# Two 128-token tiles taken one after the other through norms, turns and dense products

## The chip, the cores and the metric

The kernel runs on one NeuronCore of a Trainium2 chip. Its engines run in parallel, each through its own list of instructions in order: TensorE (PE in the rows, with PEld for its weight loads), VectorE (DVE), ScalarE (ACT), GpSimd (POOL), and SyncE (SP), whose list issues most of the DMA transfers. They wait for each other through semaphores. The metric is the time of one execution on the device, in microseconds (us); for one core that is the time of that core. All data is float32.

## The reference

256 tokens of width 1024 pass two blocks and then a third. Block 0 mixes by moving averages (pool), block 1 by a gated delta rule (GDN), both followed by a squared-ReLU MLP and a gated embedding; the third has attention of several kinds, a mixture of 32 experts and a last gated embedding.

```python
for i in range(2):
    mix = pool_mixer(x, ...) if i == 0 else gated_deltanet(x, ...)
    x = layer_norm(ALPHA * x + mix, ln_gain[i, 0], ln_bias[i, 0])
    ff = square(relu(x @ mlp_w1[i])) @ mlp_w2[i]            # 1024 -> 4096 -> 1024
    pe = sigmoid(x @ ple_gate_w[i] + ple_gate_b[i]) * (p[i] @ ple_proj[i])
    x = layer_norm(ALPHA * x + ff + pe, ln_gain[i, 1], ln_bias[i, 1])
x += attention(rmsnorm(x, ln1));  x += experts(rmsnorm(x, ln2))
x += sigmoid(rmsnorm(x, ln_ple) @ gate) * (p2 @ proj);  out = rmsnorm(x, ln_f)
```

A layer norm needs the mean and variance over the 1024 values of a token, an RMS norm the mean square. Both work on each token by itself, and so does every dense product.

## The kernel before

The 256 tokens are two tiles of 128, tile 0 and tile 1, one token to a partition. `x`, `pre` and `side` are (128, 2, 1024) arrays in SBUF: partition, tile, column. `ps` is all of PSUM, four pairs of banks of 1024 columns. `ring` has six slots for weights (2 MB each), filled by SyncE; `row_buf` has three slots for a broadcast row (a gain, a bias), filled in turn by GpSimd as `row_used` lets it go.

**A norm and a turn.** A dense product wants its input with the columns on the partitions, so after a norm TensorE transposes both tiles (`pe_transpose`, L477, 8 transposes a tile) into PSUM pairs 0 and 1. Pair 0 gets columns 0 to 511 of both tiles and pair 1 the rest, so both copies to `xT` wait for tile 1: VectorE copies pair 0 (L483), ScalarE pair 1 (L487). I call this a turn. There are eight: `ln00`, `ln01`, `gdny`, `ln10`, `rn1`, `att`, `rn2`, `rnp`. In `v_layer_norm` VectorE first takes the statistics of both tiles (L430 to L432), then for each tile subtracts the mean and multiplies by the gain (L437), takes the reciprocal of the standard deviation that ScalarE made (L440), and scales and adds the bias (L441). An RMS norm has its square and root on ScalarE (L468, L469) and two VectorE steps (L456, L457).

**Dense products.** `pe_dense` (L498) multiplies `xT` by two ring slots of weights, tile 0 and then tile 1. TensorE runs a float32 product as two passes, and the trace has a record for each: 32 records of 128x512 a tile. It serves the two embedding gates (`pe_ple`, followed by the embedding product L552, 8 records a tile), GDN's and attention's output products and the last gate.

**The MLP.** Eight steps of 512 hidden columns. A step is an up product (four chunks of weights), a turn of its 128x512 squares (L668), and a down product (four chunks). Each float32 product is split into three products of fp32r halves (L591 to L593). ScalarE makes the high half of each chunk of weights (L758) and VectorE the low half (L709), into four buffers. TensorE's order is up(s+1) chunk 0, turn(s), up(s+1) chunks 1 to 3, down(s). A step's turn and the making of its halves so lie beside the next step's up product. The first step and the last have no such neighbour. In every chunk both tiles are computed.

**Order of the stages** on TensorE: pool products (L511, L520); turn, gate and embedding products, MLP of block 0; turn `ln01`, the small products for GDN's gates (L847, 16 columns), six units of GDN input products (L866, 256 columns, both tiles at once); the delta rule; turn `gdny`, GDN output product, norm and turn `ln10`, gate and embedding products, MLP of block 1; norms `ln11` and `rn1`, attention input (L1274); attention; turn `att`, output product; norm and turn `rn2`, router (L1667); experts; the last embedding product (L1764), turn `rnp`, last gate, last norm, output. The order is written out by hand in one function for each engine.

## Time and profile before

| | us |
|---|---|
| median of 3 runs (2198.16 to 2199.28) | 2199.13 |
| the profiled execution, its own time | 2196.63 |
| its span, first to last instruction | 2194.8 |
| TensorE busy (92% of the span) | 2022.3 |
| VectorE busy (32%) | 702.3 |
| ScalarE busy (19%) | 425.7 |

The mean granted clock of TensorE is 0.941 of full speed. The profiled execution is 2.50 us under the median; 1.83 us of its time lie outside its span. In a row of a timeline the first number is the start in us from the span's start, the second the duration in us (of a merged group, from its first start to its last end), then engine, line, operation, output and inputs, form and count, and in brackets the idle time of that engine before it and what ended it.

### The profile page before, as it was taken

The numbers are of one execution on the slowest core, as the hardware profiler recorded it, in microseconds if no ns is written. First come the engines' busy times: TensorE is split into PE (matmuls) and PEld (weight loads), VectorE is DVE, ScalarE is ACT, GpSimd is POOL, SyncE is SP. The second block draws the span as 40 slices with busy tenths as digits, with TensorE's granted clock in tenths as the row PEclk, the third lists the DMA queues.
The fourth block names the chain that finished last, engine by engine and source line by source line (L and its number), as shares of the span: only waits on it lengthen the run. The fifth ranks groups of instructions, "written<-read, shape, count | busy, mean of one in ns | idle before, by whom it ended". The sixth has DMA issues, their size and how long they took to land.

```text
span 2194.8 us, 22402 instructions
## 1 busy us (share of the span) xinstructions
PE 2022.3 (92%) x8722; PEld 1219.0 (56%) x8722; DVE 702.3 (32%) x980; ACT 425.7 (19%) x648; POOL 12.8 (1%) x20
## 2 busy tenths in 40 slices
PE   5899989989799996977789999999999999999997
PEld 3588778579347885866454343444435344444433
DVE  4355433275335543035221312122221221222132
ACT  1244412112124442015210011011101010101002
POOL 0000000000000000000000000000000000000000
PEclk8999979989899998967889999999999999999998
DMA  9245421300433344110448999999899999989972
GB/s 367 115 176 208 176 112 39 115 1 0 172 144 153 153 190 183 66 50 1 175 182 353 422 408 382 409 378 422 363 423 408 378 409 376 422 365 422 384 305 96
DMA packets 67807, 543.32 MB, mean 248 GB/s; under 512 B 7552, under 2 KB 7552, under 8 KB 10528
## 3 DMA queue, kind: packets, MB, share of 16 engines
q1 hardware_dynamic: 65296, 533.53, 59.7%
q0 software_dynamic: 2160, 7.87, 1.1%
q8 instruction: 44, 0.72, 0.1%
q10 hardware_dynamic: 288, 1.05, 0.1%
q14 instruction: 19, 0.16, 0.0%
HBM read 541.37 MB, written 1.05 MB: 247 GB/s over the span
## 4 chain that ended last, share of the span: by engine, by line
PE 90%; DVE 6%; ACT 2%; issue 1%; DMA 0%; DVEq 0%; SPq 0%; ACTq 0%
PE ps L1889 15%; PE ps L1875 10%; PE ps L1904 8%; PE ps L498 7%; PE ps L591 6%; PE ps L592 6%; PE ps L593 6%; PE ps L1918 5%; PE ps L866 4%; PE ps L1072 3%; PE ps L1274 3%; PE ps L1980 2%; PE ps L1967 1%; PE ps L874 1%; PE ps L1949 1%; PE ps L1279 1%
## 5 line engine op out<-in xcount | busy, mean ns | idle before, releaser
L1889 PE MATMUL ps<-ring,arena 128*64 128x512 f32 x1536 | 334.9, 594 | 0.0
L1889 PEld LDWEIGHTS ps<-ring,arena 128*64 128x64 f32 x1536 | 108.2, 137 | 214.3 <-issue 214.3
L591 PE MATMUL ps<-ring_split,arena_split 128*128 128x512 f32 x512 | 208.5, 407 | 18.4 <-DVE ring_split L709 15.8
L1875 PE MATMUL ps<-ring,arena 128*128 128x512 f32 x512 | 224.0, 596 | 0.0
L2112 DVE TENSOR_SCALAR arena<-ps 128x512 f32<-128x512 f32 x40 | 27.7, 692 | 601.7 <-PE ps L1889 344.6
L592 PE MATMUL ps<-ring_split,arena_split 128*128 128x512 f32 x512 | 206.1, 403 | 0.0
L593 PE MATMUL ps<-ring_split,arena_split 128*128 128x512 f32 x512 | 205.9, 402 | 0.0
L709 DVE TENSOR_TENSOR ring_split<-ring,ring_split 128x1024 fp32r<-128x1024 f32 x128 | 155.3, 1223 | 115.0 <-ACT ring_split L758 114.9
L1904 PE MATMUL ps<-ring,arena 128*64 128x512 f32 x768 | 170.1, 595 | 0.0
L1875 PEld LDWEIGHTS ps<-ring,arena 128*128 128x128 f32 x512 | 97.8, 191 | 117.2 <-issue 115.9
L758 ACT CAST ring_split<-ring 128x1024 fp32r<-128x1024 f32 x128 | 132.7, 1049 | 118.5 <-PE ps L593 108.0
L498 PE MATMUL ps<-ring,xT 128*128 128x512 f32 x320 | 145.2, 616 | 5.7 <-ACT xT L487 5.7
L2243 ACT ACTIVATE arena<-arena 128x512 f32<-128x512 f32 x40 | 25.2, 631 | 593.2 <-DVE arena L2112 593.2
L591 PEld LDWEIGHTS ps<-ring_split,arena_split 128*128 128x128 f32 x512 | 98.6, 193 | 44.3 <-issue 17.1
L1918 PE MATMUL ps<-ring,arena 128*128 128x512 f32 x256 | 111.9, 595 | 2.5 <-DVE x L2133 2.5
L593 PEld LDWEIGHTS ps<-ring_split,arena_split 128*128 128x128 f32 x512 | 98.5, 192 | 24.1
L592 PEld LDWEIGHTS ps<-ring_split,arena_split 128*128 128x128 f32 x512 | 98.8, 193 | 23.2
L1904 PEld LDWEIGHTS ps<-ring,arena 128*64 128x64 f32 x768 | 53.0, 137 | 104.7 <-issue 104.7
L498 PEld LDWEIGHTS ps<-ring,xT 128*128 128x128 f32 x320 | 62.9, 198 | 85.8 <-issue 79.9
L2133 DVE SCALAR_TENSOR_TENSOR x<-ps,side,x 128x512 f32<-128x512 f32 x128 | 87.0, 742 | 1.9 <-PE ps L1949 1.9
L866 PE MATMUL ps<-xT,ring 128*128 128x256 f32 x384 | 85.9, 387 | 0.9 <-DVE arena L960 0.9
L2146 DVE TENSOR_TENSOR arena_split<-ps,arena_split 128x512 fp32r<-128x512 f32 x40 | 26.9, 690 | 186.1 <-ACT arena_split L2257 186.1
(360 smaller groups left out, 1982.6 us busy)
## 6 DMA issues: line engine op xcount, KB each, us to landing
ring<-experts_dram SPq DMA_DIRECT2D x384, 1024.0 KB, 10.7
ring<-weights_dram SPq DMA_DIRECT2D x57, 2048.0 KB, 9.0
row_buf<-rows_dram POOLq DMA_DIRECT2D x15, 512.0 KB, 5.8
ring<-weights_dram SPq DMA_DIRECT2D x3, 1024.0 KB, 11.6
tab<-tables_dram SPq DMA_DIRECT2D x1, 2285.0 KB, 17.9
x<-tokens_dram SPq DMA_DIRECT2D x1, 1024.0 KB, 5.0
arena<-rows_dram SPq DMA_DIRECT2D x2, 512.0 KB, 19.0
xT<-weights_dram SPq DMA_DIRECT2D x1, 1024.0 KB, 7.0
```

Source lines behind the costliest of these rows:

```text
L498: m = T.matmul(ps[:, pair_of[t], half * 512:half * 512 + 512], xT[:, k, t * P:(t + 1) * P], ring[:, slot, at:at + 512], start=(k == 0), st ...
L591: T.matmul(out_, high, w_high, start=start, stop=False, skip_group_check=True)
L592: T.matmul(out_, high, w_low, start=False, stop=False, skip_group_check=True)
L593: return T.matmul(out_, low, w_high, start=False, stop=stop, skip_group_check=True)
L709: V.tensor_tensor(low, raw, high, ALU.subtract).then_inc(sem("mlp_low"), 1)
L758: A.copy(split_buffer(MLP_SPLIT_SLOT, buffer)[0], raw).then_inc(sem("mlp_high"), 1)
L866: m = T.matmul(ps[:, n % 4, b * SEQ:(b + 1) * SEQ], w[:, k * STEP + b * P:k * STEP + (b + 1) * P], xT[:, k, :], start=(k == 0), stop=(k == ...
L1875: ins = T.matmul(bank(2 * half_ + m), xs_big[:, 2 * c + d, :], w[:, d, m * STEP:(m + 1) * STEP], start=False, stop=c == 3 and d == 1, skip ...
L1889: ins = T.matmul(bank(first_bank + m)[at:at + SMALL], xs_small[:, 2 * c + d, SMALL * (j - 1):SMALL * j], w[half_][:, d, m * STEP:(m + 1) * ...
L1904: ins = T.matmul(bank(to)[at:at + SMALL], actT[:, 0, f % 4, SMALL * (f // 4):SMALL * (f // 4 + 1)], w[:, d, half_ * STEP:(half_ + 1) * STE ...
L1918: ins = T.matmul(bank(4 + half_), actT[:, f // 4, f % 4, :], w[:, d, half_ * STEP:(half_ + 1) * STEP], start=f == 0, stop=f == 7, skip_gro ...
L2133: V.scalar_tensor_tensor(out=part, in0=bank(banks[i]), scalar=weight_s[:, t, bass.ds(k, 1)], in1=part, op0=ALU.mult, op1=ALU.add).then_inc ...
```

## The change

Everything that stood between two big products for both tiles now goes tile by tile, with semaphores of their own for each tile (`norm_x0`, `norm_x1` and so on).

- **Turns.** `pe_transpose` puts tile t into PSUM pair t. Tile 0 is copied by ScalarE alone, in two copies of 512 columns; tile 1 by VectorE (first half) and ScalarE (second half).
- **Norms.** `v_layer_norm` finishes tile 0 before it begins tile 1, the sum before the norm (`produce`) among it. For `ln11` the following RMS norm of tile 0 is put between.
- **Products.** Dense products of tile 0 start when tile 0 is turned. The first unit of GDN's and of attention's input product is done as 128 + 128 columns instead of 256; GDN's small products come after its first unit.
- **Embedding product.** In block 0 it comes before the gate products, right behind the pool products, and its weights are loaded ahead of the gate's; in block 1 between tile 0's and tile 1's gate products.
- **MLP.** First up product: tile 0's four chunks, then tile 1's. It no longer waits for the embedding's result (`ple_side`), only for tile 0's gate sum. The last turn comes in the middle of the last-but-one down product. The last down product does tile 0's four chunks, then tile 1's.
- **Pool residual.** `ALPHA*x + b*s` is computed ahead of the pool products, and the product is multiplied by the scale instead (same value, one VectorE pass over a tile fewer behind it).
- **GDN end.** Tile 0's output norm is done before tile 1's sum; that sum's PSUM pair is 3 instead of 2.
- **End.** Tile 0's last norm and its store go ahead of tile 1's sigmoid.

The core of the diff (the norms' and products' callers change as the list says):

```diff
+            sp.dma_start(pleT[:], ple_in).then_inc(sem("ple_loaded"), 16)
             fill(sp, "gate00", 2)
...
+        def v_layer_norm(v, tag, produce, gain, bias, meanwhile=None):
+
+            for t in range(TILES):
+                produce(t)
...
+                    g, b = row(v, gain), row(v, bias)
+                elif meanwhile is not None:
+                    meanwhile()
+                v.wait_ge(sem(f"norm_var{t}"), count(LAYER_NORMS, tag))
+                V.scalar_tensor_tensor(out=pre[:, t, :], in0=pre[:, t, :], scalar=mv[:, t, 0:1], in1=g,
...
+        def pe_transpose(pe, t, src, ready, least):
+
+            pe.wait_ge(sem(ready), least)
+            for c in range(KT):
+                m = T.transpose(ps[:, t, c * P:(c + 1) * P], src[:, t, c * P:(c + 1) * P], ident)
+                if c % 4 == 3:
+                    m.then_inc(sem(f"T{t}_psum"), 1)
...
+        def a_transpose(a, tag, t):
+            for half_ in range(2):
+                if t == 0 or half_ == 1:
+                    a.wait_ge(sem(f"T{t}_psum"), 2 * count(TURNS, tag) - 1 + half_)
+                    A.copy(*half_turned(t, half_)).then_inc(sem(f"T{t}"), 1)
+
...
+            v.wait_ge(sem("x_loaded"), 16)
+            link(v, V.tensor_tensor(pre[:, 0, :], b, s, ALU.mult))
+            for t in range(TILES):
+                m = V.scalar_tensor_tensor(out=side[:, t, :], in0=x[:, t, :], scalar=ALPHA, in1=pre[:, 0, :],
+                                           op0=ALU.mult, op1=ALU.add)
+            link(v, m)
+            return s
+
+        def v_pool(v, s, t):
+
+            v.wait_ge(sem("pool_psum"), t + 1)
+            V.tensor_tensor(pre[:, t, :], ps[:, 2 + t, :], s, ALU.mult).then_inc(sem("pool_read"), 1)
+            v.wait_ge(sem("pool_read"), t + 1)
+            link(v, V.tensor_tensor(pre[:, t, :], pre[:, t, :], side[:, t, :], ALU.add))
+            if t == TILES - 1:
+                v.sem_inc(sem("row_used"), 2)
...
+        def pe_gate(pe, tag, t, gate_slots):
+            pe_transpose(pe, t, x, f"norm_x{t}", count(NORMS, tag))
+            pe_turned(pe, tag, t)
+            pe_dense(pe, "ple_gate_psum", t, gate_slots, t)
...
+            def first_up():
+
+                pe.wait_ge(sem("ple_logit"), TILES * layer + 1)
+                for t in range(TILES):
+                    for c in range(4):
+                        m = up_tile(weights_of(c, c), c, t)
+                        if t == 1:
+                            m.then_inc(sem("mlp_product"), 1)
+                        elif c == 3:
+                            m.then_inc(sem("mlp_first"), 1)
+
...
+            def last_down(s, par):
+
+                pe.wait_ge(sem("mlp_hid_low"), 8 * layer + s + 1)
+                for t in range(TILES):
+                    for c in range(4):
+                        m = down_tile(par, weights_of(down_chunk(s, c) - 4, c), c, t, last=True)
+                        if t == 1:
+                            m.then_inc(sem("mlp_product"), 1)
+                        elif c == 3:
+                            m.then_inc(sem("mlp_last"), 1)
 
...
-            step(MLP_STEPS - 2, 0)
-            turn(MLP_STEPS - 1, 1)
-            down(MLP_STEPS - 1, 1, last=True)
+            s = MLP_STEPS - 2
+            up(s + 1, (0,))
+            turn(s, 0)
+            up(s + 1, (1, 2, 3))
+            down(s, 0, chunks=(0, 1))
+            turn(s + 1, 1)
+            down(s, 0, chunks=(2, 3))
+            last_down(s + 1, 1)
...
+            w = take(pe, GDN_IN_SLOTS[0])
+            for t in range(TILES):
+                pe_transpose(pe, t, x, f"norm_x{t}", count(NORMS, "ln01"))
+                pe_turned(pe, "ln01", t)
+                for b in range(4):
+                    at = b * SEQ + t * P
+                    for k in range(KT):
+                        m = T.matmul(ps[:, 0, at:at + P], w[:, k * STEP + b * P:k * STEP + (b + 1) * P],
+                                     xT[:, k, t * P:(t + 1) * P], start=(k == 0), stop=(k == KT - 1))
+            m.then_inc(sem("gdn_in_psum"), 1)
             pe.wait_ge(sem("small_loaded"), 16)
...
-            v.wait_ge(*flag("gdn_o1_psum"))
-            V.tensor_tensor(O[:, 1, :], O[:, 1, :], ps[:, 2, :], ALU.add).then_inc(sem("gdn_o"), 1)
             v.wait_ge(sem("gdn_zw"), 1)
             normed(0)
+            v.wait_ge(*flag("gdn_o1_psum"))
+            V.tensor_tensor(O[:, 1, :], O[:, 1, :], ps[:, 3, :], ALU.add).then_inc(sem("gdn_o"), 1)
...
-            a_transpose(a, "rnp")
+            a_transpose(a, "rnp", 1)
             for t in range(TILES):
                 a.wait_ge(sem("ple_gate_psum"), TILES * 2 + t + 1)
                 A.activation(pre[:, t, :], ps[:, 2 + t, :], ACT.Sigmoid).then_inc(sem("ple_gate"), 1)
-            a_rms_norm(a, "rnf", "last_x", 0)
-            for t in range(TILES):
-                a.wait_ge(sem("norm_x"), before(NORMS, "rnf") + t + 1)
+                a_rms_norm(a, "rnf", t, "last_x", t + 1)
+                a.wait_ge(sem(f"norm_x{t}"), count(NORMS, "rnf"))
                 a.dma_start(out[:, t, :], pre[:, t, :]).then_inc(sem("out_stored"), 16)
...
-            pe_ple(pe, "ln00", 0, (2, 3), 5, 2048, proj_taken=True)
+            pe_proj(pe, 0, 5, 2048)
+            for t in range(TILES):
+                pe_gate(pe, "ln00", t, (2, 3))
...
-            pe_ple(pe, "ln10", 1, (2, 3), 5, 0)
+            for t in range(TILES):
+                pe_transpose(pe, t, pre, "gdn_y", t + 1)
+                pe_turned(pe, "gdny", t)
+                pe_dense(pe, "gdn_out_psum", 2 + t, (4, 5), t)
+            pe_gate(pe, "ln10", 0, (2, 3))
+            take(pe, 5)
+            pe_proj(pe, 1, 5, 0)
+            pe_gate(pe, "ln10", 1, (2, 3))
```

Three places of the order as it is in the programs. First TensorE at the start, from the pool products (L520, now L526) to the MLP's first product (L591, now L614), before:

```order
L520 MATMUL ps<-ring,xT 128x256 x16
L477 MATMUL ps<-tab,x 128x128 x16
L498 MATMUL ps<-ring,xT 128x512 x32
L552 MATMUL ps<-ring,pleT 128x512 x8
L591 MATMUL ps<-ring_split,arena_split 128x512
```

and now:

```order
L526 MATMUL ps<-ring,xT 128x256 x16
L568 MATMUL ps<-ring,pleT 128x512 x8
L475 MATMUL ps<-tab,x 128x128 x8
L504 MATMUL ps<-ring,xT 128x512 x16
L475 MATMUL ps<-tab,x 128x128 x8
L504 MATMUL ps<-ring,xT 128x512 x16
L614 MATMUL ps<-ring_split,arena_split 128x512
```

The embedding product (L552, now L568) moved from behind the gates to ahead of all turns, and each tile's gate product follows its own turn.

TensorE from the delta rule's last products (into PSUM from `side`) to the MLP of block 1, before:

```order
L1163 MATMUL ps<-side,ring 128x128 x8
L477 MATMUL ps<-tab,pre 128x128 x16
L498 MATMUL ps<-ring,xT 128x512 x32
L477 MATMUL ps<-tab,x 128x128 x16
L498 MATMUL ps<-ring,xT 128x512 x32
L552 MATMUL ps<-ring,pleT 128x512 x8
L591 MATMUL ps<-ring_split,arena_split 128x512
```

and now:

```order
L1234 MATMUL ps<-side,ring 128x128 x8
L475 MATMUL ps<-tab,pre 128x128 x8
L504 MATMUL ps<-ring,xT 128x512 x16
L475 MATMUL ps<-tab,pre 128x128 x8
L504 MATMUL ps<-ring,xT 128x512 x16
L475 MATMUL ps<-tab,x 128x128 x8
L504 MATMUL ps<-ring,xT 128x512 x16
L568 MATMUL ps<-ring,pleT 128x512 x8
L475 MATMUL ps<-tab,x 128x128 x8
L504 MATMUL ps<-ring,xT 128x512 x16
L614 MATMUL ps<-ring_split,arena_split 128x512
```

The four turns and four dense products alternate, and the embedding product stands between the two gate products.

ScalarE at the end, from the copy of the embedding product to `side` to the store, before:

```order
L2335 COPY side<-ps 128x2048
L487 COPY xT<-ps 128x1024
L2339 ACT_TABLE_LOAD
L2339 ACTIVATE pre<-ps 128x1024 x2
L468 ACTIVATE pre,mv<-x 128x1024
L469 ACT_TABLE_LOAD
L469 ACTIVATE std<-mv,tab 128x1
L468 ACTIVATE pre,mv<-x 128x1024
L469 ACTIVATE std<-mv,tab 128x1
L2343 DMA out_dram<-pre 128x1024 x2
```

and now:

```order
L2416 COPY side<-ps 128x2048
L494 COPY xT<-ps 128x4x128
L2420 ACT_TABLE_LOAD
L2420 ACTIVATE pre<-ps 128x1024
L468 ACTIVATE pre,mv<-x 128x1024
L469 ACT_TABLE_LOAD
L469 ACTIVATE std<-mv,tab 128x1
L2423 DMA out_dram<-pre 128x1024
L2420 ACT_TABLE_LOAD
L2420 ACTIVATE pre<-ps 128x1024
L468 ACTIVATE pre,mv<-x 128x1024
L469 ACT_TABLE_LOAD
```

Tile 0's two turn copies (L494) stand right ahead of the first row now, so the copy of `side` (128x2048) moved behind them, and for tile 1 a sigmoid, a square, a table load and a root follow each other where the table was loaded once before.

## Rows read from the trace of the kernel before

**Rows 1.** The page's chain of waits that ended last, shares of the span by engine.

```profile
PE 90%; DVE 6%; ACT 2%; issue 1%; DMA 0%; DVEq 0%; SPq 0%; ACTq 0%
```

**Rows 2.** Waits of TensorE: who for whom, us in total, times, longest.

```profile
PE ps L477 <- DVE x L441: 29.1, 6, 12.0
PE ps L591 <- DVE ring_split L709: 15.8, 4, 4.3
```

**Rows 3.** Timeline of the start, TensorE.

```profile
17.87 7.14 PE L520 MATMUL ps<-ring,xT 128*128 128x256 f32 x32 [1.20 <-ACT xT L2477]
...
42.77 29.81 PE L498 MATMUL ps<-ring,xT 128*128 128x512 f32 x64 [1.30 <-ACT xT L487]
...
80.76 0.50 PE L591 MATMUL ps<-ring_split,arena_split 128*128 128x512 f32 x1 [1.31 <-DVE side L567]
```

**Rows 4.** DMA landing: row_buf issued at 1.9 us (L422), ring issued at 4.3 us.

```profile
DMA to landing us min/median/max: 12.4/12.4/12.4
...
ring<-weights_dram SPq DMA_DIRECT2D x1, 2048.0 KB, 28.6
```

**Rows 5.** Timeline: the first norm and turn behind the MLP of block 0.

```profile
280.56 2.36 DVE L751 TENSOR_TENSOR pre<-ps,side 128x1024 f32<-128x1024 f32 x2 [10.87 <-PE ps L593]
282.95 0.69 DVE L430 BATCH_NORM_STATS2 stats<-pre 128x6 f32<-128x512 f32 x1
...
286.01 1.28 DVE L437 SCALAR_TENSOR_TENSOR pre<-pre,mv,row_buf 128x1024 f32<-128x1024 f32 x1
...
288.74 1.97 PE L477 MATMUL ps<-tab,x 128*128 128x128 f32 x8 [8.22 <-DVE x L441]
...
294.41 7.01 PE L847 MATMUL ps<-par,xT 128*128 128x16 f32 x32 [1.10 <-ACT xT L487]
...
317.90 1.57 ACT L905 ACTIVATE arena<-ps,par 128x256 f32<-128x256 f32 x4 [11.05 <-PE ps L866]
```

**Rows 6.** By line and form: ScalarE's copy of 512 columns out of PSUM.

```profile
L2247 ACT COPY arena<-ps 128x512 f32<-128x512 f32 x40 | 23.6, 590 | 7.9 <-PE ps L1926 7.9
```

**Rows 7.** Timeline of the MLP of block 0: its first step's end, its last step.

```profile
92.26 1.29 DVE L725 TENSOR_SCALAR xT<-ps 128x512 f32<-128x512 f32 x2 [7.08 <-PE ps L593]
...
261.81 1.04 PE L668 MATMUL ps<-tab,xT 128*128 128x128 f32 x8
...
266.43 0.77 PE L591 MATMUL ps<-ring_split,arena_split 128*128 128x512 f32 x1 [3.58 <-DVE ring_split L709]
```

**Rows 8.** Stretches: TensorE, its loads, VectorE, ScalarE, GpSimd, clock, DMA share, GB/s.

```profile
96.00:98.00 2.00, 1.45 (x4) 1.19 (x5) 2.00 (x3) 2.00 (x3) 0.00 (x0) 0.50 0.03 8
...
296.00:298.00 2.00, 2.00 (x11) 2.00 (x11) 0.00 (x0) 0.00 (x0) 0.00 (x0) 0.50 0.21 84
```

**Rows 9.** The chain in time: TensorE in the delta rule, 128x128 products.

```profile
473.80 62.57 PE ps L1072 x544
```

**Rows 10.** Timeline: GDN's end and the way to the MLP of block 1.

```profile
553.70 1.23 DVE L1204 TENSOR_TENSOR ring<-ring,arena 128x1024 f32<-128x1024 f32 x1
...
563.53 30.55 PE L498 MATMUL ps<-ring,xT 128*128 128x512 f32 x64 [1.10 <-ACT xT L487]
...
644.41 0.50 PE L591 MATMUL ps<-ring_split,arena_split 128*128 128x512 f32 x1 [1.31 <-DVE side L567]
```

**Rows 11.** Timeline behind the MLP of block 1, TensorE.

```profile
856.36 3.42 PE L477 MATMUL ps<-tab,pre 128*128 128x128 f32 x16 [12.53 <-DVE pre L457]
...
860.88 24.44 PE L1274 MATMUL ps<-xT,ring 128*128 128x256 f32 x112 [1.10 <-ACT xT L487]
```

**Rows 12.** Timeline behind attention: the router.

```profile
1093.10 5.42 PE L1667 MATMUL ps<-par,xT 128*128 128x32 f32 x32 [1.10 <-ACT xT L487]
```

**Rows 13.** Timeline of the end.

```profile
2154.48 1.87 ACT L2335 COPY side<-ps 128x2048 f32<-128x2048 f32 x1 [5.32 <-PE ps L1764]
...
2157.31 27.73 PE L498 MATMUL ps<-ring,xT 128*128 128x512 f32 x64 [1.12 <-ACT xT L487]
...
2187.16 1.28 ACT L469 ACT_TABLE_LOAD   x1
```

342 lines of the change are left out of this document (176 added, 166 removed).

## Prediction

> **What bounds the kernel now.** I read the chain of waits first: TensorE holds 90% of it, VectorE 6%, ScalarE 2%, DMA nothing [rows 1]. So the time is TensorE's work plus the gaps in which it stands. Then TensorE's own waits: 29.1 us in six waits for the output of a layer norm, 15.8 us in four waits for halves of MLP weights [rows 2]. Last the timeline at each place that the change touches. The half of the span that the experts take is not touched, and I look for every gain ahead of them, in gaps that the same pattern makes: both tiles are finished before either goes on.
>
> **The prices.** One tile of a layer norm is, on VectorE, the sum ahead of it (1.2, half of 2.36), the statistics (1.53, half of 286.01 − 282.95) and 2.73 from the mean's subtraction to TensorE's start [rows 5]: with 0.2 from TensorE's end to the first step it is 5.7 us. Eight transposes take 1.04 at full clock [rows 7] and 1.97 at half [rows 5]; a copy of 512 columns takes 0.59 [rows 6]. A turn of one tile costs TensorE 1.04 + 0.59 + 0.15 for signals = 1.8 us, 2.7 at half clock. A dense product is 27.7 us for 64 records at full clock [rows 13], so 13.85 a tile, and the embedding product's 16 equal records 6.9. 48 fp32r products take 11.3 (80.76 to 92.26 less 0.2) [rows 3, 7].
>
> **1. Start to the MLP of block 0.** Before, the pool products end at 25.0, the gates run from 42.77 to 72.6, and the MLP begins at 80.76 [rows 3]. Now VectorE makes `ALPHA*x + b*s` ahead of its copy to `xT`. That needs `pool_scale`, which lands at 1.9 + 12.4 = 14.3 [rows 4]; three passes of 1.25 and the copy's 1.2 let the pool products start at 19.4 instead of 17.87: 1.5 us later, ending at 26.5. Tile 0's norm starts at 23.1 with two passes (2.5) in place of one, with 1.3 for the table load that stood there before as well, and ends at about 30; only then comes tile 1's multiply (31.3), which frees the second half of the embedding product, so that ends at 34.8. Turn: 36.7. The weights of the gate's second half (gate01) landed at 32.9 before [rows 4]; now embedding weights and inputs go ahead of them, about 1.8 MB or 6 us in that trace's queue, so 39.5 at the latest; the first 8 records run until 40.1 without them. Then gate, turn, gate: 36.7 + 27.7 + 1.8 = 66.2, and the up product follows at once, since its halves are made beside tile 1's gate. Gain 80.8 − 66.2 = 14.6. Bounds: 8 if gate01 comes 6 us later than I think, 16 if nothing waits.
>
> **2. The first step of each MLP.** TensorE waited 4.3 us there at the longest [rows 2]. The first of the two relu passes (0.65, half of 1.29 [rows 7]) now lies beside tile 1's product. Twice 0.6 = 1.2.
>
> **3. The last step of each MLP.** TensorE stands 3.58 us at 266.43 [rows 7], and 48 products run from there to 280.4 (0.2 ahead of 280.56 [rows 5]), 14.0 us instead of 11.3, since the clock had fallen. With the last turn 24 products (5.6) earlier, ScalarE's copy (1.0) and VectorE's difference and first low half (2.5) are ready before the products end, and the remaining halves come one each 1.2 us against 1.4 of product. Wait and slow clock both go: 3.6 + 2.7 = 6.3, twice = 12.6. The bounds are 7.2 (the wait alone) and 12.6.
>
> **4. Behind the MLP of block 0.** From 280.4 to unit 0's end 317.7 (0.2 ahead of 317.90) are 37.3 us [rows 5]. Now tile 0's norm (5.7) lies beside tile 1's last 24 products (5.6), so TensorE turns it at 0.1. Then 1.8 + 64 passes of 128 columns at 0.115 ([rows 9], 62.57/544) = 7.4, again 1.8 + 7.4 for tile 1, whose norm (5.7 behind the end) is ready by 9.3, and the small products: 7.0 at half clock [rows 5], 3.9 at full. Sum 22.4, gain 14.9. The small products ran throughout at half clock and did not raise it (0.50 in the middle of them [rows 8]). So it may fall again while they run. Behind that the next unit starts slow, at up to 2.5 us; I take 0.9, and 14.0.
>
> **5. GDN's end to the MLP of block 1.** Tile 0's output norm started at 553.70, behind tile 1's sum [rows 10]. Ahead of it, its two steps end 1.8 us earlier, at 554.4. Turn: 556.3. Then dense, turn, dense, turn, gate, embedding product, turn, gate: 4 × 13.85 + 3 × 1.8 + 6.9 = 67.7, end 624.0. Tile 0's layer norm lies beside tile 1's dense product; tile 1's norm, ready 5.7 behind 585.8, beside tile 0's gate. Before, the MLP began at 644.41 [rows 10]: gain 20.4. Bounds: 17 with a fallen clock at 556, 21.
>
> **6. Behind the MLP of block 1.** Two norms follow each other here. TensorE waited 12.53 from 843.8 to 856.36 and ended unit 0 at 860.88 + 64 × 0.218 = 874.8, 31.0 us behind [rows 11]. Now tile 0's layer norm is done at 0.1, its RMS norm waits behind tile 1's sum and statistics (2.9) and ends at 4.4. Turn, 7.4, turn, 7.4: 22.8, gain 8.2. TensorE stands 4.4 us and its clock probably falls; before it was back at full as the unit began. That costs 0.9 in the turn and some 2.3 in products: 5.0 to 8.2, I take 6.2.
>
> **7. Behind attention.** Each tile's turn of `att` now stands ahead of its own product, where one turn stood: no gain. Of `rn2` tile 0's norm lies beside tile 1's product, so tile 1's is transposed at about 1090.0 and the router starts near 1091, not 1093.1 [rows 12]; 2.0 of gain, 0 to 3.
>
> **8. The end.** ScalarE began its 1.87 copy of `side`, on which the gate waits, at 2154.48 [rows 13]. Now tile 0's two half copies (1.2) stand ahead, and wait for its first transposes (about 2155.0): the gate starts at 2158.0, 0.7 later. Tile 1's root now stands behind a table load of 1.28 of its own [rows 13]; the earlier store of tile 0 gives back some 0.5. Loss 1.5.
>
> **Sum**, against the profiled execution's 2196.63 (span 2194.8): 14.6 + 1.2 + 12.6 + 14.0 + 20.4 + 6.2 + 2.0 − 1.5 = 69.5, so 2127.1. The median of the runs is 2.5 above that execution: 2199.13 − 69.5 = 2129.6, rounded 2129.5.
>
> **Rivals.** *The clock.* After the 4.33 us wait at 92 the trace shows TensorE at 1.2 GHz (0.50 at 96 to 98 [rows 8]), and 48 products behind such a wait took 2.7 us more. The change makes 16 turns of one tile out of eight of both. If 13 of them, all but the three whose wait stays long anyway, let the clock fall, that is 13 × 2.4 = 31 less: 2160.5. Against it: a turn's gaps are under 1 us each, with 1 us of transposes between. [...]
>
> *The norms are not covered.* If ScalarE, in order, holds tile 1's root behind tile 0's copies until TensorE gets to that turn, tile 1 comes late, and a norm of 5.7 stands open once in each of terms 1, 4, 5 and 6: 22.8 less, 2152.5. For it: the order on ScalarE is just this. Against it: in each stage the turn of tile 0 ends before tile 1's statistics do.
>
> *More than forecast.* If the clock also holds in terms 4 and 6 and in the first steps (twice 2.3 there), 7.5 more: 2122.
>
> *Slower.* The divided work stays at 1.2 GHz throughout: five dense products (27.7 more each) and two units (14 more each) are 166 us; less the 70 gained, 2296. It decides once the clock stays low over four tenths of that work. Against it, a tile's product is 13.85 us without a break, and unit 0 of GDN and the gates come back to full within 6 us of such work in this trace.
>
> **How the numbers follow.** Forecast 80%, clock 7%, norms not covered 6%, more 6%, slower 1%. The forecast's own range is 2120 to 2142, from the bounds of the terms. The clock elsewhere adds to both sides: attention and the delta rule run with many short waits, and a shifted start can give or take some us. To leave two in ten outside, the range goes to 2117 and 2147. 0.2%, which is 4.4 us, is about what a measurement here tells from no change; faster than that 0.98, within it 0.01, slower 0.01.
>
> **What would show it.** The MLP's first product at about 66 and 1.2 us less waiting behind it; no wait ahead of the last down products, and these at full clock; GDN's unit 1 about 21 us behind the last MLP product's end; 68 us from the first `gdny` turn's end to the MLP of block 1; a table load between tile 1's square and root at the end. The forecast fails if TensorE's wait for `x` stays above 10 us in total, if the granted clock shows 0.5 in the gate products, or if a wait for DMA appears at the gate of block 0.

## The result, and the profile after

| | before | after |
|---|---|---|
| median of 4 runs each, us | 2199.20 (2198.16 to 2199.95) | 2134.36 (2133.14 to 2139.90) |
| ratio of the times | | 0.9713, 95% interval 0.9696 to 0.9730 |
| the profiled execution, us | 2196.63 | 2139.90 |
| its span | 2194.8 | 2138.0 |
| TensorE busy | 2022.3 (92%) | 2016.0 (94%) |
| granted clock, mean | 0.941 | 0.951 |

The kernel is 2.9% faster: 64.8 us between the medians, 69.5 forecast. The execution that was profiled is the slowest of its four, by 5.5 us over their median; that of before was 2.6 under its own. So the two traces differ by only 56.7. The forecast time was 2129.5, 4.9 under the median.

The chain of waits of the kernel after, by engine. TensorE had 90% and VectorE 6% before [rows 1]:

```profile
PE 92%; DVE 4%; ACT 2%; issue 1%; DMA 0%; DVEq 0%; SPq 0%; ACTq 0%
```

TensorE's waits at the places of the change (line, what released it: us in total, times, the longest). Of the 29.1 us for a layer norm's output [rows 2] 0.3 are left, and two of the four long waits for MLP weights are gone:

```profile
PE ps L475 <- DVE pre L456: 7.9, 2, 4.3
PE ps L614 <- DVE ring_split L770: 7.5, 2, 3.7
PE ps L475 <- DVE pre L1690: 7.4, 1, 7.4
PE ps L504 <- ACT xT L494: 5.5, 8, 0.7
PE ps L475 <- DVE pre L1277: 2.3, 1, 2.3
```

The start, timeline (start, duration, engine, line, idle time before it). This answers to [rows 3]: the MLP's first product came at 80.76, now at 67.54. What was not foreseen is the pool products' 8.83 us behind a wait of 2.62; they took 7.14 before.

```profile
19.41 8.83 PE L526 MATMUL ps<-ring,xT 128*128 128x256 f32 x32 [2.62 <-DVE xT L2521]
...
38.55 3.70 PE L504 MATMUL ps<-ring,xT 128*128 128x512 f32 x8 [0.72 <-ACT xT L494]
...
67.54 0.79 PE L614 MATMUL ps<-ring_split,arena_split 128*128 128x512 f32 x1
```

Behind the MLP of block 0, which answers to [rows 5]: the first turn stands 0.26 us behind the last product where it stood 8.2, and the small products (L918) run at full clock, 3.64 instead of 7.01.

```profile
260.89 1.06 PE L475 MATMUL ps<-tab,x 128*128 128x128 f32 x8 [0.26 <-DVE x L442]
262.68 7.41 PE L911 MATMUL ps<-xT,ring 128*128 128x128 f32 x64 [0.73 <-ACT xT L494]
...
278.88 3.64 PE L918 MATMUL ps<-par,xT 128*128 128x16 f32 x32
```

From GDN's end to the MLP of block 1, which answers to [rows 10]. Every turn between dense products costs 1.7 us (1.8 forecast), but the first product runs 16.98 instead of 14.00. The turn ahead of it still ran at full clock (1.09); the window from 522.6 to 526.1 (the last fence, columns as in [rows 8]) shows the low clock, 0.50, in the product:

```profile
520.79 1.09 PE L475 MATMUL ps<-tab,pre 128*128 128x128 f32 x8 [2.29 <-DVE pre L1277]
522.61 16.98 PE L504 MATMUL ps<-ring,xT 128*128 128x512 f32 x32 [0.73 <-ACT xT L494]
539.42 1.04 PE L475 MATMUL ps<-tab,pre 128*128 128x128 f32 x8
541.14 14.00 PE L504 MATMUL ps<-ring,xT 128*128 128x512 f32 x32 [0.67 <-ACT xT L494]
...
592.59 0.80 PE L614 MATMUL ps<-ring_split,arena_split 128*128 128x512 f32 x1
```

```profile
522.60:526.10 3.50, 3.49 (x4) 1.52 (x5) 2.15 (x3) 1.22 (x2) 0.00 (x0) 0.50 0.00 0
```

Behind attention, which answers to [rows 12]. Before, one turn of both tiles took 3.67 and the 64 records behind it 27.73:

```profile
1053.34 3.67 PE L477 MATMUL ps<-tab,pre 128*128 128x128 f32 x16 [7.41 <-DVE pre L1617]
1058.11 27.73 PE L498 MATMUL ps<-ring,xT 128*128 128x512 f32 x64 [1.10 <-ACT xT L487]
```

Now a turn takes 1.97 and the first 32 records 15.67, and the router's products take 6.87 instead of 5.42:

```profile
993.63 1.97 PE L475 MATMUL ps<-tab,pre 128*128 128x128 f32 x8 [7.41 <-DVE pre L1690]
996.27 15.67 PE L504 MATMUL ps<-ring,xT 128*128 128x512 f32 x32 [0.68 <-ACT xT L494]
...
1031.91 1.97 PE L475 MATMUL ps<-tab,pre 128*128 128x128 f32 x8 [3.54 <-DVE pre L456]
1033.67 6.87 PE L1741 MATMUL ps<-par,xT 128*128 128x32 f32 x32
```

The end, which answers to [rows 13]. ScalarE copies `side` behind tile 0's copies, and a table load of 1.28 us is in the tail:

```profile
2097.39 1.88 ACT L2416 COPY side<-ps 128x2048 f32<-128x2048 f32 x1
2099.32 27.73 PE L504 MATMUL ps<-ring,xT 128*128 128x512 f32 x64 [1.62 <-ACT side L2416]
...
2130.67 1.06 ACT L468 ACTIVATE pre<-x 128x1024 f32<-128x1024 f32 x1 [2.55 <-DVE x L2406]
...
2131.83 1.28 ACT L469 ACT_TABLE_LOAD   x1
```

Stage by stage, each length read from the same instruction to the same instruction in both traces:

| stage | before | after | gain | forecast |
|---|---|---|---|---|
| start to MLP 0 (term 1) | 80.8 | 67.5 | 13.2 | 14.6 |
| both MLPs (2, 3) | 399.2 | 386.5 | 12.7 | 13.8 |
| MLP 0 to the `gdny` turn (4, and 1.8 of 5) | 275.7 | 260.2 | 15.6 | 15.8 |
| `gdny` turn to MLP 1 (rest of 5) | 88.2 | 71.8 | 16.4 | 18.6 |
| MLP 1 to the attention loop (6) | 138.6 | 131.4 | 7.2 | 6.2 |
| attention loop, code unchanged | 70.95 | 76.27 | −5.3 | 0 |
| `att` turn to the experts (7) | 50.3 | 52.1 | −1.8 | 2.0 |
| experts, code unchanged | 1041.4 | 1040.1 | 1.3 | 0 |
| end (8) | 49.7 | 52.2 | −2.5 | −1.5 |
| sum | 2194.8 | 2138.0 | 56.8 | 69.5 |

So four things ask for a cause: 4.9 us missing in terms 1 to 5, the sign of term 7, 1.0 more lost in term 8, and 5.3 us lost in a loop that the change does not touch.

This table is of the slowest execution of the four. x4 below has the same code up to its last 10 us, and its profiled execution ran at 2133.09, near the median here. In it terms 1 to 6 gained 69.1 in all, where 69.0 were forecast: against the table 1.2 more in the MLPs, 0.8 behind MLP 0, 1.4 from the `gdny` turn to MLP 1 and 0.8 behind MLP 1. Its attention loop was as long as here (76.6).

### The profile page after: what moved, and what is told of

It reads as the page before. It is cut to its first block, busy times and chain, and to the rows that moved or that the text cites. A ratio compares the mean times of both kernels' runs of the same rounds, so it can differ in the third digit from the quotient of the medians.

```text
span 2138.0 us, 22686 instructions
## 1 busy us (share of the span) xinstructions
PE 2016.0 (94%) x8850; PEld 1218.5 (57%) x8850; DVE 700.5 (33%) x981; ACT 433.3 (20%) x666; POOL 12.9 (1%) x20
## 4 chain that ended last, share of the span: by engine, by line
PE 92%; DVE 4%; ACT 2%; issue 1%; DMA 0%; DVEq 0%; SPq 0%; ACTq 0%
PE ps L1963 16%; PE ps L1949 10%; PE ps L1978 8%; PE ps L504 7%; PE ps L614 6%; PE ps L616 5%; PE ps L615 5%; PE ps L1992 5%; PE ps L937 3%; PE ps L1143 3%; PE ps L2054 2%; PE ps L1342 2%; PE ps L2041 1%; PE ps L945 1%; PE ps L2023 1%; PE ps L1347 1%
## 5 line engine op out<-in xcount | busy, mean ns | idle before, releaser
L614 PE MATMUL ps<-ring_split,arena_split 128*128 128x512 f32 x512 | 206.7, 404 | 7.5 <-DVE ring_split L770 7.5
L1949 PEld LDWEIGHTS ps<-ring,arena 128*128 128x128 f32 x512 | 97.8, 191 | 117.2 <-issue 115.9
L614 PEld LDWEIGHTS ps<-ring_split,arena_split 128*128 128x128 f32 x512 | 97.3, 190 | 31.4 <-issue 8.8
L1992 PEld LDWEIGHTS ps<-ring,arena 128*128 128x128 f32 x256 | 48.0, 190 | 61.5 <-issue 57.4
```

Of the source, the lines that this page charges most:

```text
L614: T.matmul(out_, high, w_high, start=start, stop=False, skip_group_check=True)
L1949: ins = T.matmul(bank(2 * half_ + m), xs_big[:, 2 * c + d, :], w[:, d, m * STEP:(m + 1) * STEP], start=False, stop=c == 3 and d == 1, skip ...
L1992: ins = T.matmul(bank(4 + half_), actT[:, f // 4, f % 4, :], w[:, d, half_ * STEP:(half_ + 1) * STEP], start=f == 0, stop=f == 7, skip_gro ...
```

## The experiments

Each ran five times, with a profile. A ratio is always to the kernel before on the same chip (medians 2196.5 to 2196.8 there); "against after" is its difference from 0.9713, times 2196.6. Since both ratios are uncertain by 0.15%, such a difference is good to some 5 us, and below that only stage lengths in the traces tell.

| run | ratio (95% interval) | against after, us |
|---|---|---|
| x1 late turn | 0.9777 (0.9763 to 0.9790) | +14.1 |
| x2 pairs | 0.9774 (0.9759 to 0.9789) | +13.4 |
| x3 copy first | 0.9709 (0.9695 to 0.9723) | −0.9 |
| x4 end load | 0.9709 (0.9696 to 0.9722) | −0.9 |
| x5 before, early turn | 0.9949 (0.9936 to 0.9963) | −11.2 against before |
| x6 embedding behind gates | 0.9744 (0.9730 to 0.9757) | +6.8 |
| x7 filled waits | 0.9690 (0.9672 to 0.9708) | −5.1 |
| x8 filled attention, 12 | 0.9743 (0.9730 to 0.9756) | +6.6 |
| x9 `att` turn together | 0.9701 (0.9685 to 0.9716) | −2.6 |
| x10 late turn, filled | 0.9731 (0.9715 to 0.9747) | +4.0 |
| x11 combination | 0.9628 (0.9607 to 0.9649) | −18.7 |
| x12 combination, attention 6 | 0.9598 (0.9584 to 0.9612) | −25.3 |

### x1: the last turn late again

```diff
-            down(s, 0, chunks=(0, 1))
+            down(s, 0)
             turn(s + 1, 1)
-            down(s, 0, chunks=(2, 3))
```

> The kernel after, but TensorE turns the last step's hidden layer of each MLP where the kernel before did, behind all the down products of the step before; the products of the last step stay divided by tile. My theory (term 3): ScalarE's copy and VectorE's first halves lie open again, TensorE waits some 3.6 us at both places and the 48 products behind each run partly at 1.2 GHz (14.0 instead of 11.3 us): 2 x 6.3 = 12.6 us slower than the kernel after, each MLP's stage 198 to 199 us long instead of 192.4. Rival A (the wait alone; the clock does not fall with it): 2 x 3.6 = 7.2 slower. Rival B (what shortened the MLP was the division by tile, not the place of the turn): within 2 us of the kernel after.

The MLP stages are 198.4 and 198.5 us long, against 193.1 and 193.4 in the profile of after (190.7 to 193.4 in the other traces with that code). The wait of [rows 7] is back at its old length:

```profile
253.24 0.76 PE L614 MATMUL ps<-ring_split,arena_split 128*128 128x512 f32 x1 [3.58 <-DVE ring_split L769]
```

10.5 us by the stages of these two traces (10.4 to 12.8 against the others), 14.1 by the ratios: term 3 is shown, and it is the place of the turn that makes it, not the division by tile.

### x10: the same wait, filled

The edit of x1, and this line:

```diff
             turn(s + 1, 1)
+            pe_warm(ps[:, 0, 0:P], 30)      # 30 transposes of ident, result unused
```

> The kernel with the late last turn once more (turn behind all down products of the step before), now with 30 idle transposes in the wait behind that turn. It splits term 3's price. My theory: of the 6 us that each MLP lost with the late turn 3.6 are the wait and 2.4 the clock that falls in it; with the wait filled the clock stays and each stage takes 196 us instead of 198.5, so 4.8 us faster than with the late turn alone, 8 to 10 us slower than the kernel after. Rival (all 6 are halves of weights that come late, at any clock): no gain from filling, 198.5.

`pe_warm(out, n)` is n times `T.transpose(out, ident, ident)`. Behind them TensorE waits 0.31 us, and the products start at full clock (0.47 and then 0.40 us a record, where x1 had 0.76 and 0.63):

```profile
253.67 0.47 PE L618 MATMUL ps<-ring_split,arena_split 128*128 128x512 f32 x1 [0.31 <-DVE ring_split L774]
```

The stages are 196.8 and 196.0 us long: filling the wait with useless work made the MLPs 1.6 and 2.5 us shorter. So of the 5.3 that a late turn costs in these traces about 2 are the clock and the rest the wait. The whole ran 10.1 us faster than x1 by the ratios, where 4.8 were expected; 4.2 of that stand in the MLPs, the others in stages whose code both kernels share, and no run shows them to be the filling's.

### x5: that part alone, in the kernel before

```diff
-            step(MLP_STEPS - 2, 0)
-            turn(MLP_STEPS - 1, 1)
+            up(MLP_STEPS - 1, (0,))
+            turn(MLP_STEPS - 2, 0)
+            up(MLP_STEPS - 1, (1, 2, 3))
+            down(MLP_STEPS - 2, 0, chunks=(0, 1))
+            turn(MLP_STEPS - 1, 1)
+            down(MLP_STEPS - 2, 0, chunks=(2, 3))
```

> The kernel before with one part of the change alone: TensorE turns the last step's hidden layer of each MLP between the two halves of the down products of the step before. My theory: the wait of 3.6 us and the fallen clock of the last step go here as they do in the whole change, with nothing divided by tile: each MLP's stage 193 to 194 us long instead of 199.6, together 11 to 13 us faster than the kernel before. Rival (it needs the division by tile, since the remaining halves of the weights come only one each 1.2 us): the wait is spread over the products, under 5 us faster. Beside it this run shows the attention loop once more in a kernel whose code behind block 1 is that of before: theory A (the 76.4 us that the loop takes in the changed kernel, against 70.95 before, are a matter of how the clock happens to fall in a run) expects anything from 70 to 77; theory B (the change itself makes the loop longer) expects 71.

Both MLP stages are 193.1 us instead of 199.8 and 199.4, and the whole is 11.2 faster. The window of the first MLP (length, TensorE busy, weight loads, VectorE, ScalarE, GpSimd, clock, DMA share, GB/s):

```profile
79.50:272.60 193.10, 188.74 (x832) 152.36 (x832) 96.21 (x87) 80.92 (x86) 0.00 (x0) 0.98 0.46 182
```

A sixth of the whole gain comes from moving one turn, with nothing divided. Its attention loop took 72.7, neither 71 nor over 76: more on this below.

### x2: both tiles turned together

```diff
             for t in range(TILES):
                 pe_transpose(pe, t, pre, "gdn_y", t + 1)
+            for t in range(TILES):
                 pe_turned(pe, "gdny", t)
```

and so at `ln00`, `ln01`, `ln10` and `att`.

> The kernel after with one thing undone: at five turns (ln00, ln01, gdny, ln10, att) TensorE transposes tile 1 right behind tile 0, and only then begins tile 0's products; norms, products and copies stay one tile at a time on the other engines. My theory (terms 1, 4, 5): the statistics, norm and scaling of tile 1 lie open at each turn. At ln00 tile 1 is ready at 40.2, 2 to 4 us of loss; at ln01 5.7 behind the last MLP product, 3.5 of loss and up to 2.5 for the clock; at gdny 4 us behind tile 0; at ln10 5.7, less 1.8 for one turn that no longer stands apart, and up to 2.5 for the clock; at att nothing. Together 13 to 20 us slower than the kernel after. Rival (the gain came from VectorE and ScalarE going tile by tile, and the order on TensorE is worth nothing): within 3 us of the kernel after.

13.4 us slower. By stages: start +2.4, MLP 0 to `gdny` +5.6, `gdny` to MLP 1 +9.3, and 2.1 less at `att`. At `ln01`, `gdny` and `ln10` the second turn waits for tile 1 and runs at 1.2 GHz (1.97 for eight transposes); at `ln00`, behind a wait of 2.44, it took 1.18:

```profile
267.78 1.97 PE L475 MATMUL ps<-tab,x 128*128 128x128 f32 x8 [4.28 <-DVE x L442]
...
535.08 1.97 PE L475 MATMUL ps<-tab,pre 128*128 128x128 f32 x8 [6.02 <-DVE pre L1280]
...
571.38 1.97 PE L475 MATMUL ps<-tab,x 128*128 128x128 f32 x8 [4.72 <-DVE x L442]
```

At `gdny` tile 1's turn began 7.1 us behind tile 0's (535.08 and 527.96), where 4 were expected. The order on TensorE is needed: norms by tile with the turns of both tiles together leave 13.4 us of the gain undone.

### x9: the `att` turn alone together again

The same edit at `att` only.

> The kernel after with the att turn alone undone: TensorE transposes both tiles of the attention's output ahead of tile 0's product. My theory of the step that failed (term 7): both tiles of the output are ready together, so a turn between the two products covers nothing and costs its own 1.0 + 0.7 us; undone, the stretch from the att turn to the router falls from 40.0 to 37.9 us, 2 us faster than the kernel after. Rival (it is the clock behind the 7.4 us wait that makes the stretch long, and the order does not matter): 40 in either order, no change.

From the `att` turn to the router 38.1 us instead of 40.0. The turns take 3.67 again and the 64 records 28.47 in one piece:

```profile
990.42 3.67 PE L475 MATMUL ps<-tab,pre 128*128 128x128 f32 x16 [7.41 <-DVE pre L1690]
993.88 28.47 PE L504 MATMUL ps<-ring,xT 128*128 128x512 f32 x64
```

The whole is 2.6 faster by the ratios, whose intervals overlap, so only the stage shows it.

### x3: the copy ahead of the residual

```diff
             link(v, V.tensor_tensor(pre[:, 0, :], b, s, ALU.mult))
+            v.wait_ge(sem("pool_T_psum"), 1)
+            V.tensor_copy(xT[:, 0:4, :], view(ps[:, 0, :], (4, SEQ))).then_inc(sem("pool_T"), 1)
             for t in range(TILES):
                 m = V.scalar_tensor_tensor(out=side[:, t, :], ...
...
             s = v_pool_residual(v)
-            v.wait_ge(sem("pool_T_psum"), 1)
-            V.tensor_copy(xT[:, 0:4, :], view(ps[:, 0, :], (4, SEQ))).then_inc(sem("pool_T"), 1)
```

> The kernel after, but VectorE's copy to xT stands between b*s and the two passes ALPHA*x + b*s, not behind them. My theory of the 1.9 us that are missing at the start: the pool products waited 2.62 us for that copy and began at 1.2 GHz (8.83 instead of 7.1 us), which delays everything to the MLP. Then they begin at 18.0 instead of 19.4 and take 7.1, and the MLP's first product comes at 65 to 65.5 instead of 68.1: 2.5 to 3 us faster than the kernel after. Rival A (the second gate unit's DMA is the next to be late): at most 1 us faster, with a wait for DMA in gate products. Rival B (the two passes only move and hold tile 0's norm back): no change.

```profile
15.61 1.23 DVE L537 COPY xT<-ps 128x1024 f32<-128x1024 f32 x1
...
17.77 7.15 PE L526 MATMUL ps<-ring,xT 128*128 128x256 f32 x32 [1.19 <-ACT xT L2570]
27.12 7.11 PE L570 MATMUL ps<-ring,pleT 128*128 128x512 f32 x16 [2.21 <-DMA pleT<-ple_in_dram]
```

The pool products start at 17.77 and take 7.15, and the MLP's first product comes at 64.81, 2.7 earlier than in after. The gates wait for no DMA, but the embedding product now does: it stands 2.21 us for its input, and it is done by 34.1, where in after its second half ended at 36.8. The whole moved by 0.9 in the ratios, which with their intervals neither confirms nor denies 2.7.

### x6: the embedding product behind the gates

```diff
-            pe_proj(pe, 0, 5, 2048)
             for t in range(TILES):
                 pe_gate(pe, "ln00", t, (2, 3))
+            pe_proj(pe, 0, 5, 2048)
```

> The kernel after with the embedding product of block 0 behind both gate products, as the kernel before had it. My theory: in the gap it cost TensorE nothing; behind the gates its 7 us stand on the path, the gates begin only 4 to 5 us earlier at most, since tile 0's norm is ready at 32.1, and tile 0's turn and the first gate products run at 1.2 GHz behind an empty 4 us. MLP's first product at 73 to 75 instead of 67.5: 5.5 to 7.5 us slower than the kernel after. Rival (the gap closes by itself: without the embedding product tile 0's gate begins at 33.5 and everything else with it): within 2 us of the kernel after.

```profile
30.54 1.06 PE L475 MATMUL ps<-tab,x 128*128 128x128 f32 x8 [3.97 <-DVE x L442]
32.33 17.00 PE L504 MATMUL ps<-ring,xT 128*128 128x512 f32 x32 [0.73 <-ACT xT L494]
```

The whole is 6.8 slower, but my 73 to 75 for the MLP's first product missed: it is 71.2, since tile 0's gate already began at 32.3 and not at 35. Its turn, behind an empty 3.97 us, took 1.06, at full clock; the gate product behind it paid, 17.00 instead of 14.00. The pool products took 7.15 here, behind a wait of 1.98, and not the 8.83 of after. So the start is 3.6 us longer, and that holds 3.0 of low clock in the gate and 1.7 that the pool products gave back. Of the other 3, 2.0 stand between MLP 0 and `gdny` (262.1, with 260.2 in after) and 1.3 from the `att` turn to the router (41.3 and 40.0). The code of both is that of after; other traces with it have 259.3 to 262.1 and 39.1 to 41.2 there, so it need not be the edit's.

### x7: waits filled with idle transposes

```diff
+            pe_warm(ps[:, 0, 0:P], 18)      # ahead of gdny; 36 ahead of rn1, 30 ahead of att
             for t in range(TILES):
                 pe_transpose(pe, t, pre, "gdn_y", t + 1)
```

> The kernel after with idle transposes of a constant matrix on TensorE ahead of three turns, where it waits anyway: 18 ahead of tile 0's gdny turn (wait 2.3 us), 36 ahead of rn1 (wait 4.3 us), 30 ahead of att (wait 7.4 us). My theory of the missing microseconds in terms 5 and 6: TensorE falls to 1.2 GHz in these waits, and the turn and the products behind it pay. With the waits filled the 32 products behind gdny take 14.0 instead of 16.1 to 17.6, tile 0's unit behind rn1 7.4 instead of 9.96, and the att turn and product 15.0 instead of 17.6: 5 to 8 us faster than the kernel after. Rival A (the clock falls later and for other reasons, or the idle work moves the fall elsewhere): 0 to 2 faster. Rival B (the idle work runs longer than the waits): slower.

```profile
519.17 2.13 PE L481 MATMUL ps<-tab 128*128 128x128 f32 x18
521.62 1.09 PE L475 MATMUL ps<-tab,pre 128*128 128x128 f32 x8 [0.32 <-DVE pre L1281]
523.44 14.00 PE L508 MATMUL ps<-ring,xT 128*128 128x512 f32 x32 [0.72 <-ACT xT L498]
...
783.51 4.09 PE L481 MATMUL ps<-tab 128*128 128x128 f32 x36
788.00 1.06 PE L475 MATMUL ps<-tab,pre 128*128 128x128 f32 x8 [0.40 <-DVE pre L456]
789.79 7.41 PE L1362 MATMUL ps<-xT,ring 128*128 128x128 f32 x64 [0.73 <-ACT xT L498]
```

The product behind `gdny` takes 14.00 instead of 16.98, and tile 0's unit behind `rn1` 7.41. The stages: `gdny` to MLP 1 68.8 (71.8), MLP 1 to the loop 128.2 (131.4), `att` turn to the router 37.5 (40.0). 8.6 us by the stages against the profile of after, 5.1 by the ratios. The wait is filled and the product behind it regains 3.0 us, so the low clock took what was missing in term 5.

### x8: the attention loop filled

```diff
+                h = head_of(branch, r, 0)
+                for _ in range(12):
+                    T.matmul(ps[:, 3, HD * h:HD * h + HD], ident, ident[:, 0:HD], start=True, stop=True)
                 pe.wait_ge(sem("att_probT"), n + 1)
```

> The kernel after with idle products of 64 columns of a constant in the attention loop: 12 ahead of each of the twelve steps' value products, where TensorE waits 0.7 to 2 us for ScalarE's copy, and 24 ahead of the first step (wait 3.6 us). My theory: the loop's length is set by the granted clock (0.58 to 0.76 in the kernel after, 0.76 to 0.91 before, 76.3 against 70.95 us); held at full clock it falls to 64 to 69 us, 7 to 12 us faster than the kernel after. Rival A (the loop is bound by ScalarE's and VectorE's steps at full clock, and the idle work only fills): 70 to 72 us, some 5 faster. Rival B (the clock stays low and each idle product costs double): 12 x 1 us and more slower.

Ahead of the first step stand 24 idle transposes more. The clock was full throughout, and the loop took 79.2 us, 3 more than in after. I had taken 12 products for 12 records; each float32 product is two:

```profile
928.31 2.89 PE L1595 MATMUL ps<-tab 128*128 128x64 f32 x24
```

2.89 us in each step is more than the 2.0 that TensorE waits. None of the expected numbers came. The window of the loop says that the clock part of mine held; that the size of the filling was wrong is shown by x12, below:

```profile
915.50:987.20 71.70, 70.89 (x625) 65.23 (x624) 33.00 (x69) 33.41 (x110) 0.00 (x0) 1.00 0.01 1
```

### x4: the table load of the end

```diff
                 A.activation(pre[:, t, :], ps[:, 2 + t, :], ACT.Sigmoid).then_inc(sem("ple_gate"), 1)
+                if t == TILES - 1:
+                    A.activation(mv[:, t, 0:1], eps(EPS6), ACT.Sqrt, bias=eps(EPS6))
```

> The kernel after, with one small square root of a constant on ScalarE right behind tile 1's sigmoid, so that the change of table stands beside VectorE's two passes. My theory (term 8): the table load of 1.28 us between tile 1's square and its root is on the path that ends the kernel; it goes, and the time from TensorE's last product to the end of the span falls from about 11 to 9.7 us: 1.3 faster. Rival (the load was beside VectorE's work anyway, or the square then waits for the small root): 0 to 0.3. In both cases the whole kernel's difference lies near what a measurement can tell, so the stage's length in the trace decides.

```profile
2122.70 1.28 ACT L2422 ACT_TABLE_LOAD   x1
2123.99 0.29 ACT L2422 ACTIVATE mv<-tab 128x1 f32<-128x1 f32 x1
2125.23 1.06 ACT L468 ACTIVATE pre<-x 128x1024 f32<-128x1024 f32 x1 [0.94 <-DVE x L2406]
...
2126.41 0.29 ACT L469 ACTIVATE std<-mv,tab 128x1 f32<-128x1 f32 x1
```

The load lies beside VectorE's passes (2122.71 to 2125.20), and the root follows the square at once. From the last sigmoid's start to the span's end 9.8 us (2131.4 − 2121.65) instead of 10.9 (2138.0 − 2127.09), so 1.2 less, as expected.

### x11 and x12: together

x11 is x3, x4, x7 and x9 in one kernel and 28 idle transposes between the two `rn2` turns. x12 adds the filling of x8 with 6 products in each step.

> The kernel after with what the runs before point to: the copy to xT ahead of the two passes at the start (2.7), the table loaded beside VectorE's passes at the end (1.2), idle transposes in the waits ahead of gdny, rn1 and att (4 to 8), both tiles' att turns together (2), and 28 idle transposes in the 3.5 us wait between the two rn2 turns, so that the router's products take 5.4 instead of 6.9 (2). If the terms add up, 11 to 16 us faster than the kernel after, 2118 to 2123 beside 2196.5 for before. Rival (clock and attention give part of it back): 5 to 8 faster.

> The kernel of the combination, and 6 idle products in each attention step instead of the 12 that the run with idle work in the loop had, with the 24 ahead of the first step. There the clock was full throughout, but 24 records a step took 2.89 us and the loop 79.2. My theory: 12 records take 1.45 us, less than the 2.0 us that TensorE waits there at full clock, so the step keeps its 4.6 to 5.1 us and the loop takes 65 to 68 us: 3 to 9 us faster than the combination alone. Rival (the step at full clock is bound by the chain through VectorE, ScalarE and the value products, which idle work always lengthens): 72 or more, no gain.

x11 ran at 2113.70 us, 18.7 faster than after by the ratios, more than the 11 to 16 expected. x12 ran at 2109.11 (2108.37 to 2110.70): ratio to before 0.9598, 1.2% faster than the change itself. Its loop took 65.3 us at full clock, and the router's products 3.66 where they took 6.87. The 30 transposes ahead of `att`, at full clock now, took 3.44 us where they took 5.81 in x7; 4.13 us of the wait stayed empty, and the `att` turns of both tiles took 3.36, where x7 had 1.09 for one:

```profile
909.30:968.20 58.90, 56.35 (x492) 50.33 (x492) 33.01 (x69) 33.66 (x112) 0.00 (x0) 1.00 0.00 1
```

```profile
1006.16 3.22 PE L481 MATMUL ps<-tab 128*128 128x128 f32 x28
1009.86 1.09 PE L475 MATMUL ps<-tab,pre 128*128 128x128 f32 x8 [0.48 <-DVE pre L456]
1010.79 3.66 PE L1754 MATMUL ps<-par,xT 128*128 128x32 f32 x32
```

### The attention loop in all traces

The loop's code is the same in all but x8 and x12. Its length (first score product to the `att` turn) goes with the clock granted in it, though not strictly (x10 and x1):

| kernel | clock | us |
|---|---|---|
| before, x7, x11 | 0.81 | 70.9 to 71.0 |
| x5 | 0.75 | 72.7 |
| x2, x6, x9 | 0.69 to 0.71 | 73.6 to 73.8 |
| x10 | 0.68 | 76.2 |
| after, x3, x4, x1 | 0.63 to 0.65 | 75.6 to 76.6 |
| x12 (filled) | 1.00 | 65.3 |

This is the window of the loop in after:

```profile
917.40:983.50 66.10, 54.34 (x302) 44.45 (x301) 33.00 (x69) 32.82 (x110) 0.00 (x0) 0.65 0.00 1
```

The kernel before and x5, which keeps its code around the loop, have 70.95 and 72.7; the eight kernels with the changed code and nothing filled between the MLPs and the loop have 73.6 to 76.6. x7 and x11 have the changed code and the short loop, but also idle transposes ahead of `gdny` and `rn1`. So the changed code can have the short loop; that it does not make it longer where nothing is filled is not shown. Why one execution is granted more than another stays open: each kernel was profiled once.

## Why the prediction was right

The time was right because the two largest causes were read rightly, norms of both tiles in front of a turn and the late last turn of each MLP, and each had its own price.

- **Term 3 (12.6)** measured 12.7 together with term 2, and 13.0 in x5 alone. The split was a wait of 3.6 and 2.7 of clock; x10 gives 1.6 and 2.5 for the clock. Term 2 (1.2): the two waits of the first step fell from 4.33 to 3.73 as forecast, but x5, which keeps them at 4.33, has MLP stages as short (193.1). So no stage length shows its 1.2.
- **Term 4 (14.0)** and the 1.8 of term 5: 15.6. From the MLP's end to the end of the small products it took 21.9, forecast 22.4. The small products ran at full clock (3.64), and the unit behind them paid some 1.6 of low clock, the case for which 0.9 had been kept.
- **Term 5 (20.4)** fell short by 2.2. The sum of products and turns was right: x7, with the wait filled, took 68.8 from the turn's start, where the forecast had 69.5 (67.7 and the first turn's 1.8). What failed is the step "end 624.0", which counted the first dense product at 13.85. It took 16.98. The term gained 18.2, between its lower bound, 17 "with a fallen clock", and 20.4; eight traces without the filling have 15.47 to 17.05 there, so the fall was no accident of one execution, and the forecast should have counted it.
- **Term 1 (14.6)** fell short by 1.4. The start of the pool products was right (19.41, forecast 19.4). Their end was counted at full clock behind a wait of 2.62 us (26.5; the next product really began at 28.07). x3 shows it: 7.15 instead of 8.83 with the shorter wait.
- **Term 6 (6.2)** was about right: the stage gained 7.2, of which 2.0 are in unchanged work long behind the first unit, which no term foresaw (luck), so 5.2, near the cold end of 5.0. x7 gives 3.1 more, the warm end of 8.2.
- **Term 7 (2.0)** had the wrong sign, −1.8, outside its bounds of 0 to 3. The step "one turn stood: no gain" and the step "the router starts near 1091" both failed. Between two tiles that are ready together a turn covers nothing (x9: 1.9 back). And before, the 3.67 of a turn of both tiles ran at the low clock and the products behind it at full (27.73; 28.47 in x9, so not wholly); a turn of one tile is over sooner, and the products pay instead (15.67, and 6.87 in the router, where it was 5.42).
- **Term 8 (−1.5)** was −2.5. The copy of `side` behind tile 0's copies cost 0.5 (the gate began 3.53 us behind its turn's start, before 3.03; 0.7 forecast), and the tail 1.2 (the load; x4 takes it away). The other 0.8 is no part of the term: the embedding product ahead of the turn took 10.19 us instead of 9.38. In the eleven other traces of the changed code that stretch was 0.8 to 1.7 us shorter than in after.

Of the rivals none happened as a whole. The clock rival priced 13 falls at 2.4 us, 31 in all. In the trace a turn with gaps of 0.7 us lost nothing (14.00 behind it at 541.14, 556.74, 579.15 and 1013.50), while waits of 2.3 to 7.4 ahead of a turn all did, in the turn or in the product behind it. The Trainium skill ("TensorE: Matmul & The Clock Gate", "HAM oscillation — how this bites in real kernels") tells of bursts of matmuls with waits for a DMA between, where each burst starts at the low clock again. The trace agrees for the waits for VectorE here that are 2.3 us and longer, and not for the gaps of 0.7. The turn alone misleads: behind the same 4.33 us ahead of `rn1` it took 1.94 in after and 1.08 in x4, but the unit behind it took 9.96 and 10.24, and 7.41 only in x7, where the wait was filled:

```profile
786.95 1.08 PE L475 MATMUL ps<-tab,pre 128*128 128x128 f32 x8 [4.33 <-DVE pre L456]
788.75 10.24 PE L1358 MATMUL ps<-xT,ring 128*128 128x128 f32 x64 [0.71 <-ACT xT L494]
```

The rival of the uncovered norms did not come: 0.3 us of waits for a layer norm's output are left. x2 prices a cousin of it, the old order on TensorE with the norms by tile: 13.4 us. Of the signs that the prediction named, the three of its failure are absent: the gate products ran at full clock (14.00 each), they waited for no DMA, and the waits for `x` are far below 10 us.

The range (2117 to 2147) was wide enough for what it left to attention, "can give or take some us": 5.3 us there in one execution. That the forecast came within 4.9 us of the median is in part luck: terms 7 and 8 missed by 4.8 together and the loop by 5.3, and against them stood 2.0 in work that no term named and 1.3 in the experts.

## What to carry to other kernels

Read, for each wait that a change removes, also the duration of the work behind it: half of what a wait costs can be a low clock, and it is regained only if no wait of such a length (2.3 to 7.4 us here) is left in its place. Judge it by the product behind the turn and not by the turn, which can still run at full clock. Divide a step by tile where the tiles become ready at different times; where they are ready together (`att` here) the division only adds a turn. Where a wait on the bounding engine can't be removed, idle transposes that fit into it brought 5 to 9 us in three places here; filling that is longer than the wait lost what it should gain, so size it from the trace, at two records for each float32 product and at the clock that the filled kernel will have.

## What the runs showed of the hardware

- The low clock behind a wait is paid by whatever comes next. Behind a turn of 16 transposes at 3.67 us the 64 records took 27.73 (before) and 28.47 (x9); behind one of 8 at 1.97 us they took 15.67 and 14.00, together 29.67 (after).
- The low clock can begin after the wait is over. The wait of 2.3 us ahead of `gdny` was followed by a turn at full clock (1.09) and a product of 15.47 to 17.05 us in eight traces, 14.00 where it was filled (x7, x11, x12).
- The pool products took 8.83 us behind waits of 2.25 us (x2) and more, and 7.15 behind 1.98 (x6) and 1.93 (x8).
- Thirty idle transposes in a wait of 3.6 us made the products behind it 1.6 to 2.5 us shorter; 18 in a wait of 2.3 us made the next product 3.0 shorter.
- The attention loop, a chain of short steps on three engines, takes 65 us at full clock and 76 at 0.65. The five times of one kernel range over 9.0 us in x7 and 10.1 in x11; over 2.3 in x12, with the loop filled, but also over 1.1 in x1, without. Whether the loop makes that range is not shown, since only one execution of each has a trace.
